# A decoder layer on one Trainium2 core: last value group and second norm re-ordered, projection split in two, residual and weights loaded in smaller pieces

## What is computed

```python
proj = x @ w_in                        # conv GLU | q | k | v | branch gates
y_conv = swish(LN(causal_depthwise_conv31(GLU(a_conv)))) @ conv_w_out
y_attn = rms_norm(differential_attention(q, k, v)) @ attn_w_o
x = LN(alpha*x + (sigmoid(g0)*y_conv + sigmoid(g1)*y_attn) @ w_out)
# product-key experts: 8 heads, 2 x 128 keys, top 16 of 16384 experts per head
h = gelu(einsum('td,thkd->thk', x, u_tab[ids])); w = softmax(best) * h
x = LN(alpha*x + einsum('thk,thkd->td', w, v_tab[ids]))      # the second norm
x = x + sigmoid(x @ ple_w_gate + ple_b_gate) * (p @ ple_w_proj)
```

## Time and profile before

| | us |
|---|---|
| median of 3 runs | 3936.49 |
| lowest and highest | 3936.02, 3939.61 |
| the profiled execution, its own time | 3941.06 |
| its span, first to last instruction | 3939.3 |
| PE busy in the span | 3877.5 (98%) |
| DVE, ACT, POOL busy | 2601.6, 1414.4, 1192.6 |
| granted TensorE clock, mean | 0.995 |
| mean DMA rate | 209 GB/s |

### The profile page before, as it was taken

The page is one execution under the profiler, slowest core; times in us unless marked ns, Lnnn a source line. Parts: engine busy times, 40 slices in busy tenths (PEclk is TensorE's granted clock), DMA queues, the critical chain, the costliest instruction groups (busy, mean ns, idle before and its releaser), DMA issues.

```text
span 3939.3 us, 58036 instructions
## 1 busy us (share of the span) xinstructions
PE 3877.5 (98%) x20433; PEld 3549.7 (90%) x20433; DVE 2601.6 (66%) x3713; ACT 1414.4 (36%) x1984; POOL 1192.6 (30%) x584
## 2 busy tenths in 40 slices
PE   8999999999998999999999999999999999999999
PEld 7888888878886889999999999999999999999777
DVE  3555555534314899577777777659888888888642
ACT  4334443341124222546446446322222222222442
POOL 4444444434442446321221221102221212122233
PEclk9999999999999999999999999999999999999999
DMA  4222222223433224587887887968887878787332
GB/s 155 97 98 99 93 93 102 97 106 132 157 120 115 96 100 152 219 332 264 315 335 263 317 334 262 375 233 322 309 298 294 308 295 298 290 312 270 116 104 77
DMA packets 206083, 822.76 MB, mean 209 GB/s; under 512 B 16944, under 2 KB 107184, under 8 KB 118576
## 3 DMA queue, kind: packets, MB, share of 16 engines
q1 hardware_dynamic: 137648, 515.62, 36.6%
q0 software_dynamic: 36864, 268.45, 17.5%
q10 hardware_dynamic: 31488, 37.76, 2.7%
HBM read 754.66 MB, written 67.11 MB: 209 GB/s over the span
## 4 chain that ended last, share of the span: by engine, by line
PE 95%; DVE 2%; ACT 2%; DMA 1%; ACTq 0%; issue 0%; DVEq 0%; SPq 0%
PE bank L604 30%; PE bank L605 30%; PE bank L606 30%; PE bank L848 2%; PE bank L647 1%; DVE sc L1366 1%; PE bank L666 1%; DMA raw<-ws 1%; PE bank L694 0%; PE bank L805 0%; ACTq L1020 0%; ACT whi L992 0%; ACT ahi L1021 0%; PE bank L684 0%; PE bank L960 0%
## 5 line engine op out<-in xcount | busy, mean ns | idle before, releaser
L992 ACT ACTIVATE whi<-raw 128x1024 fp32r<-128x1024 f32 x784 | 827.2, 1060 | 2294.3 <-PE bank L606 1715.7
L604 PE MATMUL bank<-ahi,whi 128*128 128x384 f32 (+1 forms) x3968 | 1460.1, 368 | 27.5 <-DVE alo L1315 8.1
L605 PE MATMUL bank<-alo,whi 128*128 128x384 f32 (+1 forms) x3968 | 1439.1, 363 | 0.0
L606 PE MATMUL bank<-ahi,wlo 128*128 128x384 f32 (+1 forms) x3968 | 1438.8, 363 | 0.0
L575 POOL TENSOR_TENSOR wlo<-raw,whi 128x1024 fp32r<-128x1024 f32 x316 | 790.2, 2504 | 1065.0 <-ACT whi L992 1036.3
L604 PEld LDWEIGHTS bank<-ahi,whi 128*128 128x128 f32 x3968 | 748.4, 189 | 120.3 <-issue 36.1
L606 PEld LDWEIGHTS bank<-ahi,wlo 128*128 128x128 f32 x3968 | 748.2, 189 | 77.2
L605 PEld LDWEIGHTS bank<-alo,whi 128*128 128x128 f32 x3968 | 749.0, 189 | 72.4 <-issue 0.5
L1551 DVE TENSOR_TENSOR wlo<-raw,whi 128x1024 fp32r<-128x1024 f32 x472 | 576.0, 1223 | 298.7 <-ACT whi L992 287.9
L604 PE MATMUL bank<-xwhi,whi 128*128 128x384 f32 x2048 | 685.6, 335 | 6.7 <-ACT hst L1188 6.7
L605 PE MATMUL bank<-xwlo,whi 128*128 128x384 f32 x2048 | 685.4, 335 | 0.0
(11 more groups left out here) (203 smaller groups left out, 2712.3 us busy)
## 6 DMA issues: line engine op xcount, KB each, us to landing
raw<-ws SPq DMA_DIRECT2D x394, 1024.0 KB
gelu_spill<-hst ACTq DMA_DIRECT2D x128, 192.0 KB
route_spill<-gst SPq DMA_DIRECT2D x24, 1024.0 KB
hg<-gelu_spill SPq DMA_DIRECT2D x64, 384.0 KB
hg<-route_spill SPq DMA_DIRECT2D x64, 384.0 KB
gate_spill<-gout ACTq DMA_DIRECT2D x32, 256.0 KB, 2.1
gl<-gate_spill SPq DMA_DIRECT2D x32, 256.0 KB, 2.7
xin<-xT SPq DMA_DIRECT2D x8, 512.0 KB, 8.4
```

The lines of the kernel that those rows point to most:

```text
L604: pe.matmul(ps_out, hi, xh, start=first, stop=False)
L605: pe.matmul(ps_out, hi, xl, start=False, stop=False)
L606: return pe.matmul(ps_out, lo, xh, start=False, stop=last)
L992: act.activation(whi[:, s], raw[:, s // 2, s % 2], ACT.Copy).then_inc(hi_done, 1)
```

## The change

- **Weights by blocks.** Each unit is loaded in two halves of 512 KB, each with its own semaphore (`raw_in` has four), and each half as soon as its own block has its low part. This holds for the whole program.
- **Residual by quarters.** Quarters 0 and 1 of `res` are loaded in the last units of the u product, quarters 2 and 3 in group 0 after its first and third unit load; DVE waits for one quarter at a time. `pin` (the input p, 512 KB) is loaded in group 0 too, and its split `phi`, `plo` moves from before group 0 to unit 4 of the last group.
- **Banks of the value units** are swapped, so the first unit writes 2 and 3, and PE waits for the last gelu only ahead of unit 1.
- **Rows earlier.** Unit 7 of group 0 and units 0 and 1 of group 1 also add two rows, and the last row is added in unit 3 of the last group. PE transposes `yacc` after unit 5 of that group (`turn_rows`), DVE adds it to `res` and sums it in unit 6.
- **Projection split.** Blocks 0 and 1 are projected around the variance, blocks 2 and 3 after `first_units`; the weight array has the first two gate units between the two halves of the projection. The sigmoids of the first pair come right after `first_units`.
- **A square root ahead.** `norm_squares`, which all three norms use, begins with a square root of one column.

```diff
@@ -392,16 +394,19 @@
                 nxt = sp.snap(u + 2)
-                sp.wait_ge(lo_done, 2 * u + 2)
-                sp.dma_start(raw[:, s], ws[nxt]).then_inc(raw_in[s], 16)
+                for half in range(2):
+                    sp.wait_ge(lo_done, 2 * u + (half + 1))
+                    sp.dma_start(raw[:, s, half], ws[nxt, :, half]).then_inc(raw_in[2 * s + half], 16)
...
+            for half in range(2):
+                sp.dma_start(raw[:, 0, half], ws[0, :, half]).then_inc(raw_in[half], 16)
...
+            def load_res(q):
+                sp.dma_start(res[:, 4 * q:4 * q + 4], x1_sp[:, 4 * q:4 * q + 4]).then_inc(x1_in[q], 16)
...
-                    sp.dma_start(pin[:], pT).then_inc(p_in, 16)
                 if k in (2, 4):
                     load_hg(k // 2 - 1, k // 2 - 1)
-                if k in (3, 5, 7, 11):
-                    q = (3, 5, 7, 11).index(k)
-                    sp.dma_start(res[:, 4 * q:4 * q + 4], x1_sp[:, 4 * q:4 * q + 4]).then_inc(x1_in, 16)
+                if k in (3, 7):
+                    load_res(k // 4)
...
                     load_unit(g * 8 + (B6 // 2 + k), k % 2)
+                    if first and k in (0, 2):
+                        load_res(2 + k // 2)
+                    if first and k == 6:
+                        sp.dma_start(pin[:], pT).then_inc(p_in, 16)
...
+                            w = (b + 2 * u + half) % 4
+                            mm = three(ps[u][:], whi[:, w, t], wlo[:, w, t], ahi[:, kk], alo[:, kk], kk == 0, kk == KD - 1)
...
+            def turn_rows():
+                pe.wait_ge(yacc_ok, 1)
+                for q in range(4):
+                    for k in range(4):
+                        d = slice((4 * q + k) * P, (4 * q + k + 1) * P)
+                        mm = pe.transpose(ps[4 + q][:, k * P:(k + 1) * P], yacc[:, d], ident[:])
+                mm.then_inc(yacc_full, 1)
+            def value_group(g, q, last=False):
                 for u in range(8):
                     pe.wait_ge(evac6, g * 8 + (u + 1))
                     for half in range(2):
                         b, s = g * 16 + (B6 + 2 * u + half), 2 * (u % 2) + half
+                        bank = 2 * ((u + 1) % 2) + half
...
+                            pe.wait_ge(evac5, 2 + U5)
                         pe.wait_ge(lo_done, b + 1)
                         for k in range(8):
                             if u == 0 and half == 0:
                                 pe.wait_ge(w_ok, g * 8 + (k + 1))
                             t = slice(k * P, (k + 1) * P)
-                            mm = three(ps[s][:, 0:TD], whi[:, s, t], wlo[:, s, t],
+                            mm = three(ps[bank][:, 0:TD], whi[:, s, t], wlo[:, s, t],
                                        xwhi[q][:, k], xwlo[q][:, k], k == 0, k == 7)
                         mm.then_inc(blk_done, 1)
...
-            pe.wait_ge(evac5, 2 + U5)
+                    if last and u == 5:
+                        turn_rows()
             pe.wait_ge(g_evac, 2 + TD // 4)
-            with pe.Fori(0, 8) as i:
+            with pe.Fori(0, 7) as i:
                 for q in range(2):
                     value_group(2 * i + q, q)
-            def project(n, first_bank, after=None):
-                pe.wait_ge(lo_done, B7 + n + 1)
+            value_group(14, 0)
+            value_group(15, 1, last=True)
+            def project(n, b, banks, after=None):
+                pe.wait_ge(lo_done, b + 1)
                 for j in range(4):
-                    if n == 1:
-                        pe.wait_ge(yacc_used, j + 1)
+                    if n % 2 == 1 and j == 2:
+                        pe.wait_ge(evac7, 4 * n - 2)
                     for k in range(2):
                         t = slice((2 * j + k) * P, (2 * j + k + 1) * P)
-                        mm = three(ps[first_bank + j][:], whi[:, n, t], wlo[:, n, t],
+                        mm = three(ps[banks[j]][:], whi[:, b % 4, t], wlo[:, b % 4, t],
                                    phi[:, k], plo[:, k], k == 0, k == 1)
                     if j == 1 and after is not None:
                         after()
                 mm.then_inc(blk_done, 1)
...
-            def mean_of_x2():
-                pe.wait_ge(evac7, 8)
-                norm_mean(2, msum2)
             pe.wait_ge(evac6, 2 + U6)
+            pe.wait_ge(yacc_used, 1)
             pe.wait_ge(p_ok, 1)
-            project(0, 0)
-            pe.wait_ge(yacc_ok, 1)
-            for q in range(4):
-                for k in range(4):
-                    d = slice((4 * q + k) * P, (4 * q + k + 1) * P)
-                    mm = pe.transpose(ps[4 + q][:, k * P:(k + 1) * P], yacc[:, d], ident[:])
-            mm.then_inc(yacc_full, 1)
-            project(1, 4)
-            pe.wait_ge(evac7, 4)
-            project(2, 0, after=mean_of_x2)
+            project(0, B7, (0, 1, 2, 3), after=lambda: norm_mean(2, msum2))
             norm_var(2, KD)
-            pe.wait_ge(evac7, 12)
-            project(3, 2)
+            project(1, B7 + 1, (4, 5, 0, 1))
...
+                            pe.wait_ge(evac7, KD)
...
-            first_units(B8, ln[2]["lo_ok"])
-            pe.wait_ge(evac7, KD)
+            pe.wait_ge(evac7, 8)
+            first_units(B7 + 2, ln[2]["lo_ok"])
+            project(2, B7 + 6, (4, 5, 6, 7))
+            project(3, B7 + 7, (2, 3, 4, 5))
...
+                act.wait_ge(raw_in[s], unit)
...
+                act.activation(std[:, 0:1], eps[:], ACT.Sqrt)
...
-            def take_e(n, first_bank):
+            def take_e(n, banks):
                 for j in range(4):
-                    act.copy(eT[:, 4 * n + j], ps[first_bank + j][:]).then_inc(evac7, 1)
-            for n in range(3):
-                step(B7 + n, n)
-                take_e(n, 4 * (n % 2))
+                    act.copy(eT[:, 4 * n + j], ps[banks[j]][:]).then_inc(evac7, 1)
+            step(B7, 0)
+            take_e(0, (0, 1, 2, 3))
             norm_squares(2, KD, res)
+            step(B7 + 1, 1)
+            take_e(1, (4, 5, 0, 1))
+            def next_weights(k):
+                if k == 12:
+                    step(B7 + 2, 2)
             norm_affine(2, KD, res, ahi, ACT.Identity,
                         lambda k: pv[:, V_LN2G + k:V_LN2G + k + 1], lambda k: pv[:, V_LN2B + k:V_LN2B + k + 1],
-                        between=lambda k: step(B7 + 3, 3) if k == 4 else None)
-            take_e(3, 2)
+                        between=next_weights)
             def take_y(m, s, first=False):
@@ -1286,7 +1305,19 @@
                         act.activation(sig[:, u], ps[u][:], ACT.Sigmoid,
                                        bias=pv[:, bass.ds(2 * i + (V_PLEB + u), 1)]).then_inc(evac8, 1)
-            ple_pair(0, first=True)
+            for s in range(2):
+                if s == 0:
+                    step(B7 + 3, 3)
+                act.wait_ge(blk_done, B7 + 6)
+                act.activation(sig[:, s], ps[s][:], ACT.Sigmoid, bias=pv[:, V_PLEB + s:V_PLEB + s + 1]
+                               ).then_inc(evac8, 1)
+            for s in range(2):
+                step(B7 + 4 + s, s)
+            step(B7 + 6, 2)
+            take_e(2, (4, 5, 6, 7))
+            step(B7 + 7, 3)
+            take_e(3, (2, 3, 4, 5))
+            take_y(0, 0, first=True)
             with act.Fori(1, U8 // 2 - 1) as i:
...
-            dve.wait_ge(p_in, 16)
-            dve.tensor_copy(phi[:], pin[:])
-            dve.drain()
-            dve.tensor_tensor(plo[:], pin[:], phi[:].bitcast(F32), ALU.subtract).then_inc(p_ok, 1)
...
-            dve.wait_ge(x1_in, 64)
...
+            def add_values(g, q, first=False, second=False, last=False):
...
+                    if first and u % 2 == 0:
+                        dve.wait_ge(x1_in[u // 2], 16)
...
+                        p = ps[2 * ((u + 1) % 2) + n][:, 0:TD]
...
                     if first:
-                        for n in range(max(0, 2 * (u - 3)), 2 * (u - 2) if 3 <= u < 7 else 0):
+                        for n in range(max(0, 2 * (u - 3)), 2 * (u - 2) if 3 <= u else 0):
                             add_rows(n, n // RING, n % RING, first=(n == 0))
-                    else:
-                        add_rows(8 * g + u, 2 * g + u // RING, u % RING, more=not (last and u >= RING))
+                    elif second:
+                        for n in range(10 + u + min(u, 2), 11 + u + min(u + 1, 2)):
+                            add_rows(n, n // RING, n % RING)
+                    elif not last or u < 4:
+                        add_rows(8 * g + (4 + u), 2 * g + (1 + u // RING), u % RING, more=not last)
+                    if last and u == 3:
+                        dve.drain().then_inc(yacc_ok, 1)
+                    if last and u == 4:
+                        dve.wait_ge(p_in, 16)
+                        dve.tensor_copy(phi[:], pin[:])
+                        dve.drain()
+                        dve.tensor_tensor(plo[:], pin[:], phi[:].bitcast(F32), ALU.subtract).then_inc(p_ok, 1)
```

(54 more changed lines are left out.)

6 lines of the change are left out of this document (1 added, 5 removed).

## The result

Median of the changed kernel 3951.04 us (3949.7 to 3955.27), beside it the kernel before 3938.43 (3936.02 to 3940.78); ratio 1.0033, interval 1.0022 to 1.0044. The change costs 12.6 us. The forecast was 3935.0, within 0.2% of before, in a range from 3924 to 3944; the measured time lies above the range. The profiled executions have spans of 3950.0 and 3939.3.

What follows compares the result with a forecast made beforehand. PE, busy 98% of the span, was taken as the bound, so only its waits could give time. Start and rows +0.6, end -0.8, square root -1.3, the rest 0: -1.5 us, median 3936.49 to 3935.0, range 3924 to 3944.

Steps and rivals of the forecast that it cites:

- A wait that I have at nothing appears in all 16 groups: Value groups: the sign that would prove the forecast wrong, a wait counted as zero showing up in every group.
- Start of the value groups: First value units: with banks swapped PE starts at 2612.1, not 2618.8; gain 6.2 us, 8.4 at most, 4.9 if matmuls slow.
- Rival E: Start of value groups: the bank swap brings nothing, as the new first blocks wait for data too; +5, 3940; chance 0.05.
- rival C: From 2620 to 2720 us: DMA is the bound, with 38.3 MB to move; slower, 3944; chance 0.13.
- some 20 us behind their issue: Group 0: residual quarters 2 and 3 come at units 4 and 6, that long after being issued; no cost counted.
- Rows earlier: Groups 0 and 1: two more rows put DVE behind PE; stall 6.1 us plus 0.7 for slow matmuls.
- Rival A: Groups 0 and 1: the backlog of rows isn't felt and PE loses nothing; 3928.2; chance 0.18, with PE fast in the end 0.05.
- The end: Last group and second norm: reordered work with waits near 3.7, 5 and 5 us and slow stretches; gain 0.8 us.
- rival B: The end: PE stays fast, neither block 0 nor the variance runs slow; 5.5 us less, 3929.5; chance 0.08.
- Square root ahead: Norm 1: the table load of 1.28 us leaves the path; gain 1.3 us, or 0 if ACT's idle time is shorter.
- Halved loads: Whole program: loading weights in halves gains nothing beyond what is counted elsewhere; 0, between -1 and +1 at the start.
- D: Value groups: halves move slower; at 22% less rate they take 3% longer, 30 us, 3965; chance 0.03.

Runs made afterwards that it cites:

- after_shifted: The changed kernel with 24 empty drains ahead of DVE's value loop, which then begins at instruction 1287: 3942.74 us, ratio 1.0012.
- before_shifted: The kernel before with only 17 empty drains ahead of DVE's value loop, which then begins at instruction 1263: 3942.33 us, ratio 1.0012.
- rows_late: The changed kernel with the four moved row sums put back behind the others, the end untouched: 3937.61 us, ratio 1.0.
- before_two_blocks: The kernel before with 41 empty drains ahead of DVE's value loop, which then begins at instruction 1287: 3939.04 us, ratio 1.0001.
- spread_end_reordered: rows_late_loads_spread with the last group's folds ahead of unit 6's add, and ACT's work around the projection and block 1's banks changed: 3926.45 us, ratio 0.9969.
- spread_two_blocks: spread_end_reordered with 40 drains, so that DVE's value loop lies in two instruction blocks: 3927.97 us, ratio 0.9973.
- rows_late_loads_spread: rows_late with two of the four first row gathers named behind unit 1 and residual quarters 2 and 3 issued with units 2 and 4: 3934.69 us, ratio 0.9994.

## Why the prediction was wrong, point by point

- **The step that failed most was a term put at nothing.** The sum has none for the place of DVE's code: its loop was costed as if moving instructions ahead of it were free. Four rows and four waits moved ahead of it shifted it by 17 instructions, and that cost 8.3 us (after_shifted; the same shift alone cost the kernel before 4.1 in the median and 6.2 in its turns, before_shifted). "A wait that I have at nothing appears in all 16 groups" was named as what would make it wrong; one appeared at the five returns to the loop's head. In the trace of before the sign was there to read: 1.93 us of "issue" at each head, and the 0.66 behind it.
- **Start of the value groups: gain 6.2, measured none.** PE did as forecast until 2618. Then ten of its matmuls took 0.32 us and not 0.17 (granted clock 0.72 from 2618 to 2624), so PE's 48th value matmul came at 2624.24 against 2628.51. Of these 4.3 us 0.8 come from a u product that ended sooner in this trace (its last matmul starts at 2610.92 against 2611.74), which leaves 3.5 for the swap, less than the 4.9 given as lower bound. But the sum took it for granted that DVE would have the same lead when its rows began. DVE stood at late low parts, and began as before, and PE's lead went into waits for DVE. Rival E had the result, that the swap brings nothing, though the waits lie behind units 3 to 6 and not in the first blocks; rival C had this mechanism with a wrong measure: it laid the bytes over 100 us, where there was room; the peak was from 2620 to 2655, with a share of 0.95 to 1.05 in each 5 us and 390 GB/s in the first 20. It was there before the change too (1.00 and 392), when PE came later to it. That residual quarters 2 and 3 come "some 20 us behind their issue" had only their own use in view, not whom they delay.
- **Rows earlier: cost 6.8, measured 5.1.** Right in mechanism and in the places of the waits (1.14, 1.97 and 1.67 us where 1.7, 2.4 and 2.0 were forecast); somewhat large. DVE's idle 3.36 us were gone, as counted. Rival A falls.
- **The end: gain 0.8, measured more.** In this pair 3.8. The three kernels with the end of before take 253.6, 252.3 and 251.3 us from the last value block; seven with the changed end 246.7 to 249.7; the averages are 252.4 and 248.0, so with the transposes taken off 2.4 us are gained. The waits were right; what was mis-sized is the slow stretch: block 0 and the mean took 3713.45 - 3705.46 = 8.0 us and not 9.7, the variance 16.99 and not 18.05, so the first units began 3.0 us sooner after the last value block than forecast. From there to the end 203.5 were forecast and 203.5 measured. That is part of rival B.
- **Square root ahead: gain 1.3, measured 0.1.** The forecast looked at whether the new place was free and never at whether the old one was on the path; the load was hidden behind PE's last variance pass.
- **Halved loads: 0, and none was seen.** PE has no wait for raw weights in the steady groups, and rows_late, with the halves, takes the time of before; D falls. From 3000 to 3600 ACT waits 78.9 us for raw in 21 waits (65.9 in 17 before), and the share is 0.85 at 298 GB/s (0.81 at 299): no wait of PE is put down to it.

The sum with what was measured: 0 for the start, +5.1, +8.3, -2.4 for the end, 0 for the square root: +11.0 against the 12.6 measured. The 1.6 between lie inside the intervals, and are not explained further. Against the forecast of -1.5 the sum is off by 14.1: 8.3 for the loop and 6.2 for the start, which are the two failed steps; 1.3 for the square root; 1.7 and 1.6 the other way for the rows and the end; and those 1.6.

## What to carry to other kernels

Before moving instructions ahead of a loop, look at its heads in the trace: idling put down to "issue" there means that its code doesn't stay on the engine, and a shift of a few instructions can turn a hidden fetch into a wait in each turn; idle instructions that move the head past the edge cured it here. An earlier start is worth only what its slowest supplier can follow, so lay the bytes of the change over the stretch in which the lead is to be won, not over the phase, and ask whose bytes come first. And before a setup step is moved off the path, check that it was on it.

## What the runs showed of the hardware

- A return to a loop head of DVE cost 1.9 to 2.7 us where the loop of 303 instructions began at 1246, 1247 or 1263, and nothing where it began at 1287; the instruction queue q14 moved 25 or 26 packets over five turns in the first case and none in the second. What lies behind the next edge was usable 7.9 to 8.2 us after the return in 13 of 15 returns of three kernels, and 7.0 and 7.1 us in the other two.
- The granted clock changes between traces at a place where the kernels' work is the same. The variance of norm 1, behind a wait of 1.45 us in all traces, took 15.33 us in ten of thirteen, 16.98 in before_two_blocks, and 17.86 and 17.92 in spread_end_reordered and spread_two_blocks, with a granted clock of 0.62 from 1231 to 1240 where before_shifted and rows_late_loads_spread, for instance, have 1.00. So up to 2.5 us of those two kernels' gain in the end are lost again in norm 1. There is one trace of each kernel, so whether it goes with the kernel or with the execution isn't known, and what sets it was not tried.
